# Rotary swap of a two-block transformer kernel: on-chip transfers issued by GpSimd in place of permutation matmuls

## The reference

```python
def apply_rope(x, positions):
    half = HEAD_DIM // 2
    inv_freq = ROPE_THETA ** (-jnp.arange(half, dtype=jnp.float32) / half)
    ang = positions.astype(jnp.float32)[..., None] * inv_freq
    cos = jnp.cos(ang)[:, :, None, :]
    sin = jnp.sin(ang)[:, :, None, :]
    xf = x.astype(jnp.float32)
    x1, x2 = xf[..., :half], xf[..., half:]
    return jnp.concatenate([x1 * cos - x2 * sin, x2 * cos + x1 * sin], axis=-1).astype(x.dtype)
...
    qa = apply_rope(qa.reshape(b, s, A_Q_HEADS, hd), positions).reshape(b, s, A_KV_HEADS, ra, hd)
    ka = apply_rope(ka.reshape(b, s, A_KV_HEADS, hd), positions)
...
    qb_rot = apply_rope(qb, positions).reshape(b, s, B_KV_HEADS, rb, hd)
    qb_raw = qb.reshape(b, s, B_KV_HEADS, rb, hd)
...
    ks = apply_rope(ksb.reshape(b, s, B_KV_HEADS, hd), positions)
    kw = apply_rope(kwb.reshape(b, s, B_KV_HEADS, hd), positions)
```

## Time and profile before

| | |
|---|---|
| median of 3 runs | 1698.63 us |
| span of the profiled execution | 1697.7 us, 0.93 below the median of the runs |
| PE busy | 1681.8 us, 99% |
| DVE busy | 1217.0 us, 72% |
| ACT busy | 1030.9 us, 61% |
| GpSimd busy | 694.6 us, 41% |
| weight traffic | 306.70 MB, 181 GB/s in the mean |

### The profile page before, as it was taken

How to read it: one execution, slowest core, us unless ns; L and a number is a source line. 1 busy time by engine, 2 the same in 40 slices (tenths; PEclk the granted TensorE clock), 3 DMA queues, 4 the chain that set the end, 5 groups by cost and what they waited for, 6 DMA issues and landing times.

```text
span 1697.7 us, 26081 instructions
## 1 busy us (share of the span) xinstructions
PE 1681.8 (99%) x9714; PEld 1441.0 (85%) x9714; DVE 1217.0 (72%) x1832; ACT 1030.9 (61%) x1933; POOL 694.6 (41%) x672
## 2 busy tenths in 40 slices
PE   8999999999999999999999999999999999999998
PEld 7868888889868988889888978888898888788887
DVE  7977799958868799957664757665576647576663
ACT  5687666645786766655553657554565536575543
POOL 4154166602046176506660052673066600517640
PEclk9999999999999999999999999999999999999999
DMA  8925486576807676649656636866496665357662
GB/s 242 240 72 159 135 234 192 174 223 174 208 20 207 162 204 185 214 146 248 188 185 223 202 96 155 227 177 217 142 244 182 190 227 190 108 143 218 186 211 75
DMA packets 416352, 306.70 MB, mean 181 GB/s; under 512 B 10179, under 2 KB 369013, under 8 KB 416226
## 3 DMA queue, kind: packets, MB, share of 16 engines
q1 hardware_dynamic: 415536, 304.51, 61.7%
q0 software_dynamic: 688, 0.53, 0.1%
q10 hardware_dynamic: 2, 0.00, 0.0%
HBM read 303.95 MB, written 1.05 MB: 180 GB/s over the span
## 4 chain that ended last, share of the span: by engine, by line
PE 92%; DVE 4%; ACT 1%; DMA 1%; POOL 1%; issue 1%; SPq 0%; DVEq 0%; POOLq 0%
PE bank L1537 33%; PE bank L1540 16%; PE bank L1651 9%; PE bank L1652 9%; PE bank L1653 9%; PE bank L1603 3%; PE bank L1614 3%; PE bank L1611 3%; DVE whl L959 1%; DMA raw<-in_w_in 1%; PE bank L1584 1%; PE bank L1855 1%; PE bank L1825 1%; DVE PB L1215 1%; PE bank L1573 1%; PE bank L1575 1%
## 5 line engine op out<-in xcount | busy, mean ns | idle before, releaser
L959 DVE TENSOR_TENSOR whl<-raw,whl 128x1024 fp32r<-128x1024 f32 (+2 forms) x572 | 738.8, 1315 | 171.7 <-ACT whl L593 167.1
L1537 PE MATMUL bank<-hsA,whl 128*128 128x512 f32 x2384 | 762.9, 397 | 0.7 <-DVE U L969 0.6
L593 ACT ACTIVATE whl<-raw 128x1024 fp32r<-128x1024 f32 (+2 forms) x572 | 575.4, 1029 | 161.6 <-PE bank L1653 103.9
L1540 PEld LDWEIGHTS bank<-hsA,whl 128*128 128x128 f32 x2384 | 447.9, 188 | 101.4
L1540 PE MATMUL bank<-hsA,whl 128*128 128x256 f32 x2384 | 473.0, 278 | 0.0
L1537 PEld LDWEIGHTS bank<-hsA,whl 128*128 128x128 f32 x2384 | 369.3, 189 | 6.0 <-issue 3.2
L593 ACT ACTIVATE low<-bank 128x256 f32<-128x256 f32 x390 | 145.6, 379 | 274.9 <-PE bank L1537 255.3
L1402 POOL TENSOR_TENSOR HB<-CB,UB 128x256 f32<-128x256 f32 x88 | 123.7, 1405 | 337.9 <-ACT CB L596 337.2
L1651 PE MATMUL bank<-whl,hid 128*128 128x512 f32 x528 | 205.9, 390 | 0.0
L1653 PE MATMUL bank<-whl,hid 128*128 128x512 f32 x528 | 205.4, 389 | 0.0
L1652 PE MATMUL bank<-whl,hid 128*128 128x512 f32 x528 | 205.4, 389 | 0.0
(11 more groups left out here) (227 smaller groups left out, 2033.1 us busy)
## 6 DMA issues: line engine op xcount, KB each, us to landing
raw<-in_ffn_w_up SPq DMA_DIRECT2D x176, 512.0 KB, 5.3
raw<-in_ffn_w_down SPq DMA_DIRECT2D x120, 512.0 KB, 4.6
raw<-in_w_in SPq DMA_DIRECT2D x96, 512.0 KB, 6.3
raw<-in_ffn_w_gate SPq DMA_DIRECT2D x88, 512.0 KB, 4.1
raw<-in_w_out SPq DMA_DIRECT2D x32, 512.0 KB, 4.7
raw<-in_ffn_w_down SPq DMA_DIRECT2D x24, 256.0 KB, 3.0
G<-in_norm_g SPq DMA_DIRECT2D x12, 512.0 KB, 8.1
raw<-in_cmp_w SPq DMA_DIRECT2D x8, 512.0 KB, 5.9
```

Of the source, the lines that this page charges most:

```text
L593: return nc.scalar.activation(out_, in_, func, **kw)
L959: v.tensor_tensor(wlo[c_ % RING][:, x:y], raw[:, c_ % RAW, x:y], whi[c_ % RING][:, x:y].bitcast(F32), ALU.subtract)\
L1537: return mm(out_[:, 0:2 * n], whi[slot][:, at:at + P], rhs[:, 0:2 * n], start=x == 0, stop=False, **g32)
L1540: return mm(out_[:, n:2 * n], wlo[slot][:, at:at + P], rhs[:, 0:n], start=False, stop=False, **g32)
```

## The change

The permutation matrix, its matmuls and the semaphore `swap_used` go. The eleven tiles are taken as five pairs and one single tile (pair r is tiles 2r and 2r+1 for r = 0 to 4; r = 5 is tile 12). For each of them GpSimd issues four transfers of 32 partitions from `U1` to `tm`, with the blocks exchanged, and then makes the cosine multiply of both tiles at once; DVE multiplies `tm` by `sinT` in place and adds. `tm` and `cq` keep their size, so they hold one pair. A pair's transfers wait for the add of the pair before.

```diff
-ROPE = [0, 1, 2, 3, 4, 5, 6, 7, 8, 9, 12]
-KEYS = [(4, KA), (5, KS), (12, KW)]
-
-
-def rope_step(t):
-    return 9 if t == 12 else t // 2 + 1
+ROPE = [(0, 1), (2, 3), (4, 5), (6, 7), (8, 9), (12,)]
+KEYS = [(2, KA), (2, KS), (5, KW)]
+
+
+def rope_step(r):
+    return 9 if r == 5 else r + 1
...
-                t = ROPE[r]
-                dst = U1[:, PLACE[t], :] if t < 6 or t > 9 else QR[:, t - 6, :]
-                dve.wait_ge(swap_ready, 11 * L + r + 1)
-                v.tensor_tensor(tm[:, r % 2, :], bank[6 + r % 2][:, 0:S], sinT[:, :], ALU.mult).then_inc(swap_used, 1)
-                dve.wait_ge(swap_used, 11 * L + r + 1)
-                dve.wait_ge(cosmul_ready, 11 * L + r + 1)
-                v.tensor_tensor(dst, cq[:, r % 2, :], tm[:, r % 2, :], ALU.add).then_inc(rope_done, 1)
+                t, n = ROPE[r][0], len(ROPE[r])
+                dst = U1[:, PLACE[t]:PLACE[t] + n, :] if t < 6 or t > 9 else QR[:, t - 6:t - 6 + n, :]
+                dve.wait_ge(swap_ready, 64 * (len(ROPE) * L + r + 1))
+                seq.link(v.tensor_tensor(tm[:, 0:n, :], tm[:, 0:n, :], sinT[:, :].unsqueeze(1).broadcast_to([P, n, S]), ALU.mult))
+                dve.wait_ge(cosmul_ready, len(ROPE) * L + r + 1)
+                v.tensor_tensor(dst, cq[:, 0:n, :], tm[:, 0:n, :], ALU.add).then_inc(rope_done, 1)
...
-            for r, t in enumerate(ROPE):
-                pool.wait_ge(tile_out, t0 + t + 1)
-                if r >= 2:
-                    pool.wait_ge(rope_done, 11 * L + r - 1)
-                g_.tensor_tensor(cq[:, r % 2, :], U1[:, PLACE[t], :], cosT[:, :], ALU.mult).then_inc(cosmul_ready, 1)
+            for r, pair in enumerate(ROPE):
+                t, n = pair[0], len(pair)
+                pool.wait_ge(tile_out, t0 + pair[-1] + 1)
+                if r:
+                    pool.wait_ge(rope_done, len(ROPE) * L + r)
+                for x in range(0, P, 32):
+                    pool.dma_start(tm[x:x + 32, 0:n, :], U1[x ^ 32:(x ^ 32) + 32, PLACE[t]:PLACE[t] + n, :]).then_inc(swap_ready, 16)
+                g_.tensor_tensor(cq[:, 0:n, :], U1[:, PLACE[t]:PLACE[t] + n, :], cosT[:, :].unsqueeze(1).broadcast_to([P, n, S]),
+                                 ALU.mult).then_inc(cosmul_ready, 1)
...
-                for t in ROPE:
-                    if rope_step(t) == c:
-                        r = ROPE.index(t)
-                        pe.wait_ge(tile_out, t0 + t + 1)
-                        if r >= 2:
-                            pe.wait_ge(swap_used, 11 * L + r - 1)
-                        mm(bank[6 + r % 2][:, 0:S], C("swap"), U1[:, PLACE[t], :], start=True, stop=True, **g32)\
-                            .then_inc(swap_ready, 1)
```

More of the change, by code:

```diff
@@ L41 @@
 Z_MAX = 20.0
-CONST = {"ident": 128, "swap": 128, "ntri": 128, "stick": 128, "mask_a": 256, "mask_c": 256,
+CONST = {"ident": 128, "ntri": 128, "stick": 128, "mask_a": 256, "mask_c": 256,
          "mask_cmp": 32, "count": 32, "width": 2, "freq": 1, "sign": 1, "fold": 2 * N_CMP, "heads": 8}
@@ L61, in host_constants @@
     put("ident", np.eye(P))
-    put("swap", (i[:, None] == (i ^ 32)[None, :]))
     put("ntri", np.where(i[:, None] >= i[None, :], -1.0, 0.0))
@@ L317, in build @@
     gates_ready = sem("gates_ready")
-    swap_ready, swap_used = sem("swap_ready"), sem("swap_used")
+    swap_ready = sem("swap_ready")
     cosmul_ready, rope_done, kswap_done = sem("cosmul_ready"), sem("rope_done"), sem("kswap_done")
@@ L741, in _ @@
                     ins.then_inc(cur_ready, 1)
-                for n, (t, place) in enumerate(KEYS):
-                    if rope_step(t) == c:
-                        act.wait_ge(rope_done, 11 * L + ROPE.index(t) + 1)
+                for n, (r, place) in enumerate(KEYS):
+                    if rope_step(r) == c:
+                        act.wait_ge(rope_done, len(ROPE) * L + r + 1)
                         f(KSW[HD:P, n, :], U1[0:HD, place, :], ACT.Copy)
@@ L762, in _ @@
             act.wait_ge(cmp_kv, L + 1)
-            act.wait_ge(rope_done, 11 * L + len(ROPE))
+            act.wait_ge(rope_done, len(ROPE) * (L + 1))
             for e in range(2):
@@ L1156, in _ @@
                     parameters()
-                for r, t in enumerate(ROPE):
-                    if rope_step(t) == c:
+                for r in range(len(ROPE)):
+                    if rope_step(r) == c:
                         rope(r)
@@ L1167, in _ @@
             dve.wait_ge(cmp_kv_out, L + 1)
-            dve.wait_ge(rope_done, 11 * L + len(ROPE))
+            dve.wait_ge(rope_done, len(ROPE) * (L + 1))
             v.tensor_tensor(VC[:, :, :], bank[6][:, P:P + HD].unsqueeze(1).broadcast_to([P, 8, HD]),
@@ L1713, in fold @@
                 pe.wait_ge(tile_out, p["cmp"][n][1] + 1)
-                if n == 0:
-                    pe.wait_ge(swap_used, 11 * L + len(ROPE))
                 mm(bank[7 - n][:, S:S + 2 * N_CMP], HE[:, n, :], C("fold"), start=True, stop=True, **g32).then_inc(cmp_fold, 1)
@@ L1782, in cmp_scores @@
                 ins.then_inc(cmp_z, 1)
-            pe.wait_ge(rope_done, 11 * L + len(ROPE))
+            pe.wait_ge(rope_done, len(ROPE) * (L + 1))
             pe.wait_ge(kswap_done, 3 * L + 3)
```

## The result

The changed kernel takes **1729.73 us** (median of 5 runs, 1728.76 to 1731.39) beside 1698.9 for the kernel before in the same comparison: a ratio of **1.0184** (95% interval 1.0171 to 1.0196), 31 us slower. Its profiled execution has a span of 1726.9 and a time of 1728.76, the shortest of the five. Differences within a trace are taken between profiled spans: 1726.9 - 1697.7 = 29.2 us.

A forecast was written before the change was run, and what follows sets the result against it. PE, busy 1681.8 of 1697.7 us, seemed the bound, but in layer 0 the chain was DVE's, without slack. Costs of 11.1 + 6.6 + 1.0 = +18.7 us gave span 1716.4, median 0.9 above: 1717.4 us, range 1702 to 1736.

The forecast's parts named there:

- What is removed: On PE, 22 swap matmuls of 0.43 us go: at most 9.5 us gained, only where PE is last to be ready.
- Rival (a): PE's gain is kept if landings take under 2.0 us: layer 1 keeps its 4.7, total 1692.4 us; chance 0.04.
- What is added on GpSimd: Per pair, four transfer issues of 0.54 us and one 512-column cosine multiply, which costs nothing unless the last transfer takes under 2.0.
- The landing X: Time from a pair's last transfer issue to its landing in tm: taken as 4.0 us, ends 2.6 and 5.4.
- Rival (d): Transfers queue behind weights, landing in 5.4 us or more: 35 us more, 1734 us; chance 0.08.
- Layer 0: DVE has no slack; pair 4 done at 66.8 instead of 55.72, so the layer costs 11.1 us (ends 4.1 and 18.1).
- Layer 1, "nothing lost on pair 0": Pair 0 lands before DVE comes to it; pair 4 is 8.1 us late, less 1.5 slack: cost 6.6 (ends 1.0 and 13.1).
- The last tile: Tile 12's landing delays HE: 0.9 us in layer 0 and 0.1 in layer 1, together 1.0 (ends 0 and 4).
- Edits that cost nothing: 1.4 MB more traffic per layer, ACT's key copies waiting for pair 2 and a 64 KB shorter constant: no cost.
- Rival (c), the clock: Idle TensorE runs at 1.2 instead of 2.4 GHz through a step, 5.6 us more per layer: 1728.6 us; chance 0.08.

The follow-up runs named there:

- experiment 1: The changed kernel without the transfers and their wait, the sine multiply reading its own unswapped tiles: 1697.91 us, ratio 0.9993 to the kernel before.
- experiments 2, 5 and 8: The change with two tm and cq buffers: 1723.91 us; that with pairs rotated at step r + 3, tile 12 at 11: 1707.09; that with three buffers: 1706.8.
- experiment 4: The changed kernel with each transfer cut to 64 of 256 tokens, a quarter of the bytes: 1728.82 us, ratio 1.0177 to the kernel before.
- the best form of the study: The change with PE's swap matmuls back, pairs and 512-column operations kept, two tm and cq buffers: 1696.94 us, ratio 0.9990 to the kernel before.

## Why the prediction was right, and where its terms were off

The forecast was 1717.4 (range 1702 to 1736, 0.91 for slower); 1729.73 lies in the range, 12 us above the forecast. The mechanism is the one that was forecast: the chain passes through GpSimd's transfers and `tm`, DVE waits ahead of the sine multiply, and PE waits for splits and for the compression input. Its size was +18.7 and came to +29.2. Step by step:

- **What is removed** (at most 9.5 us, counted as nothing in the sum): right, and more strongly than argued. The text allowed for the 4.7 us of layer 1 if PE set the end; experiment 1 has no transfers and gains 0.9. Rival (a), 1692.4, was out of reach in this form at any landing time: it rested on the chain of layer 1 being PE's alone, and the fastest of experiment 1's ten runs took 1695.40. A chain names the engine that was last, not by how much.
- **What is added on GpSimd** (0.54 an issue, the multiply free): 0.50 an issue. DVE never waited for the multiply, as forecast, but it was not free: where it ran beside a split of DVE's, the split took longer. At 439.69, on the chain, two halves of 816 columns took 2.98 us, and 1.92 at 48.55, where GpSimd did not multiply. In experiments 2, 5 and 8 it met DVE's rotary work as well.
- **The landing X** (4.0 taken, ends 2.6 and 5.4) is a term that was mis-sized, and its shape too: it is not one number. Layer 0 had 5.32, 1.9 (pair 1, not waited for), 1.82, 6.28 and 6.08; layer 1 had 7.27, 3.02, 4.72, 1.9 (pair 3, not waited for) and 6.19. Pair 4 was done at 67.98, so the forecast's 46.78 + 5X gives a mean X of 4.2 there, and +12.3 in place of +11.1. The ten landings on the chain have a mean of 51 / 10 = 5.1. What they go with, by and large, is the traffic beside them. Stretches between the last issue and the landing (length; busy PE, PEld, DVE, ACT, POOL; granted clock, DMA share, GB/s):

```profile
45.37:47.19 1.82, 1.82 (x11) 1.59 (x10) 0.88 (x3) 0.00 (x0) 1.79 (x3) 0.83 0.68 126
50.69:56.97 6.28, 6.28 (x37) 5.78 (x36) 3.64 (x4) 3.90 (x10) 1.79 (x3) 1.00 1.05 271
60.47:66.55 6.08, 5.75 (x32) 5.11 (x30) 0.00 (x0) 2.76 (x3) 1.80 (x3) 1.00 1.12 267
...
413.55:420.82 7.27, 7.01 (x53) 6.53 (x52) 4.15 (x5) 3.69 (x5) 1.81 (x3) 1.00 1.08 285
```

  At a share of 0.68 a pair lands in 1.8, at 0.46 (pair 3 of layer 1, 439.05 to 440.95) in 1.9, at 0.91 and 0.93 in 4.72 and 3.02, at 1.05 and more in over 6. The GB/s are all traffic of the stretch, the pair's own included. I had argued the reverse, that the loop thins the weight traffic. It does on average, but DVE's add releases GpSimd, and the split right behind the add releases SP's next load, so the two start together. In one place they did not, and the landing was short: SP issued nothing between 431.7 and 442.69, when pair 3 of layer 1 went out. No run changed the loads, so that they are the cause is argued from these rows. SP's issues in layer 0 (pair 3's last transfer went out at 50.69, pair 4's at 60.47):

```profile
50.50 2.00 SPq L462 DMA_DIRECT2D raw<-in_w_in  x2
...
59.64 1.93 SPq L462 DMA_DIRECT2D raw<-in_w_in  x2
```

  Some landings do not fit: the first, 5.32 at a share of 0.72 in its stretch, and tile 12's, with half the bytes of a pair, 5.20 at 1.01 and 5.07 at 1.08. The Trainium skill's page "DMA: Bandwidth & Descriptors" (Anatomy of one DMA) gives such a transfer about 2.15 by its fixed cost and bytes, as an estimate; the shortest rows (1.82, 1.9) come near it, and those beside weight loads do not. Rival (d), X of 5.4 or more, came true for the loaded landings and not for all.
- **Layer 0** (+11.1 in front of the last tile): +12.3 at pair 4, +12.2 at the first RHP (74.97 against 62.80). That DVE had no slack there, the argument on which all rests, was right.
- **Layer 1, "nothing lost on pair 0"**: wrong. It was to land before DVE came to it; it landed after 7.27 us, beside three chunks' loads, and DVE waited 2.49. With loops of (454.34 - 422.26) / 4 = 8.0 in place of 7.46, pair 4 is 13.0 late in place of 8.1 (422.26 is the end of pair 0's add): 2.7 of the difference stand at pair 0 and 2.2 in the loops. The first RHP is 12.9 late (461.32 against 433.44, less 15.0) and HE, counted the same way, 15.3 (476.96 against 446.64), and the layer cost 14.2. Without the 2.4 that tile 12 adds that is 11.8, where 6.6 was forecast: the largest miss, 5.2 us.
- **The last tile** (+1.0 in all): HE was 15.5 late where RHP was 12.2 in layer 0, and 15.3 where RHP was 12.9 in layer 1, so 3.3 and 2.4 more, where 0.9 and 0.1 were forecast. Its transfers landed in 5.20 and 5.07, half the bytes of a pair and no faster, as experiment 4 would have it. Moving it alone gained 2 to 4 us.
- **Edits that cost nothing**: right for the bytes (experiment 4), and for ACT's key copies in layer 0. In layer 1 it was wrong, and here a term failed that was put at nothing. The copies were to lie "inside the 6.0 us until pair 3 lands", but pair 3 landed early, and the chain ran through them. The last copy (from the chain), DVE's split and sine multiply and GpSimd's multiply (from the timelines), and the landings of pair 3 (from the view of `tm` from 436 to 444 us), whose last transfer was issued at 439.06:

```profile
438.33 0.41 ACT KSW L592
...
439.69 2.98 DVE L958 TENSOR_TENSOR whl<-raw,whl 128x816 fp32r<-128x816 f32 x2 [2.69 <-ACT whl L592]
...
443.25 0.68 DVE L1108 TENSOR_TENSOR tm<-tm,sinT 128x512 f32<-128x512 f32 x1
...
439.57 1.30 POOL L1441 TENSOR_TENSOR cq<-U,cosT 128x512 f32<-128x512 f32 x1
...
DMA to landing us min/median/max: 1.8/1.9/1.9
```

  Pair 3 had landed by about 440.9, and DVE came to it only at 443.3, because its split had waited 2.69 us for ACT, behind the copies, and then ran beside GpSimd's multiply. With the split right behind the add (ended at 437.0; 1.92 and 0.75 of work) DVE would have waited for the landing instead, so the two cost about 2.4 us, as an estimate. The kernel before had a wait of 1.82 us at the same place, where PE's lead hid it. No run moved the copies alone.
- **Rival (c), the clock**: its mechanism came, its price did not. The granted clock by stretches:

```profile
60.00:75.00 15.00, 7.22 (x37) 6.08 (x35) 8.61 (x16) 5.49 (x6) 2.27 (x3) 0.83 0.74 185
...
445.00:460.00 15.00, 6.26 (x32) 5.12 (x30) 8.50 (x17) 3.07 (x4) 3.31 (x5) 0.74 0.72 182
```

  PE was busy 7.22 of 15 us and 6.26 of 15, and the clock, 1.00 before, went to 0.83 and 0.74: part of each stretch at 1.2 GHz. The Trainium skill, "TensorE: Matmul & The Clock Gate" (Part 1), says that an idle TensorE goes back to half its clock, and the rows agree. But from 14 to 98 us and from 411 to 478 no piece of the chain is PE's: it runs through the transfers, GpSimd's issues, DVE and ACT, so a slower PE is not seen in the sum. That it cost nothing at all is argued from the chain, no run took the clock's fall away alone.

That time and forecast differ by only 12 us is in part luck: X in layer 0 was nearly right as a mean of 2 and 6, and the range was 34 us wide. By terms, 10.5 us are missing from the forecast of 18.7: about 1 in layer 0, 5 in layer 1's pairs, of which some 2.4 are the key copies and the stretched split, and 4 in tile 12.

## What to carry to other kernels

Before an operation is moved off the busiest engine, measure what its absence is worth, by a version that leaves it out: here that gained 1 us, and the best form of the study 2, both at the edge of noise, against 9.5 by counting matmuls. A small transfer on the path of this kernel, which streams weights, was not priced by its bytes. Give it a place where its reader comes several microseconds later (with two buffers that alone took 16.8 us off, 1723.91 to 1707.09), or leave the exchange on an engine that the others keep waiting anyway, as PE here; whether it also helps that no load starts at the same moment, the rows suggest and no run tested. When a wait moves, look again at what was hidden behind it, as ACT's key copies were. A second buffer alone does not hide a landing if the reader stands one step behind.

## What the hardware showed that I had not expected

- Transfers of 64 KB from SBUF to SBUF landed in 1.8 to 7.3 us within one kernel, issued the same way; at a quarter of the bytes in 1.6 to 5.7. With two buffers it was 4.1 to 7.8 from GpSimd and 4.1 to 7.0 from ACT's queue, both into `tm`.
- A multiply on GpSimd (1.3 us, both inputs in SBUF) holds up a DVE operation on two SBUF inputs for about its own length: 0.68 became 2.02, 0.69 became 2.29. In the change itself the twelve sine multiplies met no such multiply and took at most 0.694, but two splits did (2.98 for 1.92). The tile sums, with one input in SBUF and one in a bank, were not held up: two took 0.75 at 424.45 beside a GpSimd multiply from 424.84 on, as elsewhere.
